# A decoder layer on one core: the down weights of the experts move to ScalarE's queue

## The reference, cut to what matters

```
grp   = argmax of 4 group logits per token
top 2 of the 8 experts of that group, with gates
for each of the 32 experts e, for its rows x:
    hdn = silu(x @ w_gate[e]) * (x @ w_up[e])     # w_gate, w_up: 2048 x 512
    y   = hdn @ w_down[e]                         # w_down: 512 x 2048
out = sum over experts of gate * y, added to the residual; then a final RMSNorm
```

## Time and profile before

| | |
|---|---|
| median of 3 runs | 1797.7 us (1797.01 to 1799.74) |
| span of the profiled execution (the only time it shows of itself) | 1798.1 us |
| PE busy | 1391.6 us, 77% of the span |
| DVE, ACT, POOL busy | 468.6, 281.6, 75.3 us |
| bytes moved | 480.73 MB, of them 474.01 MB on q1 |
| chain that ended last | SPq 41%, PE 40%, DMA 8%, DVE 4% |

### The profile page before, as it was taken

How to read it: one execution, slowest core, us unless ns; L and a number is a source line. 1 busy time by engine, 2 the same in 40 slices (tenths; PEclk the granted TensorE clock), 3 DMA queues, 4 the chain that set the end, 5 groups by cost and what they waited for, 6 DMA issues and landing times.

```text
span 1798.1 us, 20225 instructions
## 1 busy us (share of the span) xinstructions
PE 1391.6 (77%) x7876; PEld 746.3 (42%) x7876; DVE 468.6 (26%) x1007; ACT 281.6 (16%) x602; POOL 75.3 (4%) x107
## 2 busy tenths in 40 slices
PE   4999999999999998887666756755766666766755
PEld 4887878888888544442111211211211211211111
DVE  4031365555554544140111101101101101102003
ACT  2002111111111243121101010110101101010111
POOL 1000011111111400000000000000000000000000
PEclk8999999999999899988887897987978977878787
DMA  8432332222222124959999999999999999999996
GB/s 247 141 116 94 111 88 71 71 70 70 70 70 82 47 94 138 320 190 403 394 398 399 395 402 395 401 396 397 400 395 402 395 399 398 395 401 395 402 395 246
DMA packets 204592, 480.73 MB, mean 267 GB/s; under 512 B 16725, under 2 KB 35302, under 8 KB 187654
## 3 DMA queue, kind: packets, MB, share of 16 engines
q1 hardware_dynamic: 192562, 474.01, 70.8%
q10 hardware_dynamic: 11988, 6.14, 1.4%
HBM read 478.01 MB, written 2.10 MB: 267 GB/s over the span
## 4 chain that ended last, share of the span: by engine, by line
SPq 41%; PE 40%; DMA 8%; DVE 4%; issue 3%; ACTq 2%; ACT 1%; DVEq 0%
SPq L507 20%; SPq L508 15%; PE ps L684 9%; PE ps L756 8%; SPq L512 6%; DMA ring<-in_moe_w_up_dram 6%; PE ps L766 6%; PE ps L901 5%; DMA ring<-in_moe_w_down_dram 2%; PE ps L1015 2%; PE ps L1030 1%; PE ps L989 1%; PE ps L704 1%; PE ps L783 1%; DVE oT L1479 1%
## 5 line engine op out<-in xcount | busy, mean ns | idle before, releaser
L1015 PE MATMUL ps<-ring,oT 128*32 128x512 f32 x2048 | 358.7, 840 | 282.7 <-DMA ring<-in_moe_w_up_dram 282.0
L1015 PEld LDWEIGHTS ps<-ring,oT 128*32 128x32 f32 x2048 | 68.7, 133 | 550.5 <-DMA ring<-in_moe_w_up_dram 317.2
L756 PE MATMUL ps<-xT,ring 128*128 128x256 f32 x768 | 191.5, 386 | 0.0
L684 PE MATMUL ps<-xT,ring 128*128 128x256 f32 x768 | 169.7, 384 | 13.6 <-ACT xT L1144 13.6
L1693 DVE TENSOR_TENSOR oT<-oT,ps 128x128 f32<-128x128 f32 x32 | 9.2, 288 | 643.8 <-ACT oT L1301 643.8
L684 PEld LDWEIGHTS ps<-xT,ring 128*128 128x128 f32 x768 | 147.6, 193 | 35.4 <-issue 15.0
L1030 PE MATMUL ps<-ring,oT 128*32 128x512 f32 x1024 | 123.4, 604 | 48.6 <-DMA ring<-in_moe_w_down_dram 28.6
L756 PEld LDWEIGHTS ps<-xT,ring 128*128 128x128 f32 x768 | 137.6, 193 | 16.6 <-issue 2.7
L1297 ACT COPY oT<-ps 128x512 f32<-128x512 f32 x32 | 18.8, 586 | 648.5 <-PE ps L1015 648.5
L901 PE MATMUL ps<-ring,oT 128*128 128x512 f32 x256 | 118.5, 617 | 1.7 <-DVE oT L1558 0.9
L1030 PEld LDWEIGHTS ps<-ring,oT 128*32 128x32 f32 x1024 | 30.2, 109 | 120.3 <-issue 66.9
(11 more groups left out here) (328 smaller groups left out, 1290.5 us busy)
## 6 DMA issues: line engine op xcount, KB each, us to landing
ring<-in_moe_w_gate_dram SPq DMA_DIRECT2D x128, 1024.0 KB, 14.3
ring<-in_moe_w_up_dram SPq DMA_DIRECT2D x128, 1024.0 KB, 14.4
ring<-in_moe_w_down_dram SPq DMA_DIRECT2D x128, 1024.0 KB, 15.2
ring<-in_w_in_dram SPq DMA_DIRECT2D x24, 1024.0 KB, 5.2
ring<-in_w_in_dram SPq DMA_DIRECT2D x32, 768.0 KB, 4.7
ring<-in_w_out_dram SPq DMA_DIRECT2D x16, 1024.0 KB, 5.1
res<-in_x_dram SPq DMA_DIRECT2D x2, 1024.0 KB, 6.0
out_dram<-oT SPq DMA_DIRECT2D x4, 512.0 KB, 3.0
```

The lines of the kernel that those rows point to most:

```text
L684: last = mm(ps[:, c, 0:S], wv[:, k, c * P:(c + 1) * P], xT[:, kq * KQ + k, :], start=(kq == 0 and k == 0), stop=(kq == 3 and k == KQ - 1))
L756: last = mm(ps[:, 5 + c, 0:S], wv[:, k, c * P:(c + 1) * P], xT[:, kq * KQ + k, :], start=(kq == 0 and k == 0), stop=(kq == 3 and k == KQ - 1))
L1015: last = mm(ps[c * B:(c + 1) * B, 1, :], xe[:, par, 4 * j + k, :], w[:, c // 2, k, :], start=(j == 0 and kp == 0), stop=(j == 3 and kp == ...
```

## The change: what it does

The sync engine keeps the loads of gate and up (chunks 0 to 3) of all experts. Of the down weights it keeps expert 0's (in the first eight chunks) and those of the loop for further tokens. All other down loads are issued by ScalarE: expert n's turn on ScalarE issues the four down loads of expert n+1, between the copy of the partial sums and the copy of the gathered tokens. Slots, semaphores and sizes are the same. The `m_turn` count moves from one chunk of an expert to another, since the sync engine no longer handles chunk 4 there.

```diff
             with sp.Fori(0, 7) as i:
                 for q in range(MSLOTS, MSLOTS + 4 * CHUNKS):
-                    sp.wait_ge(m_read, i * (4 * CHUNKS) + (q - MSLOTS + 1))
-                    if q % CHUNKS == 4:
-                        sp.sem_inc(m_turn, 1)
                     s = (q + LEAD) % MSLOTS
-                    load_chunk(s, bass.ds(i * 4 + q // CHUNKS, 1), q % CHUNKS, m_ring[s])
+                    if q % CHUNKS < 4:
+                        sp.wait_ge(m_read, i * (4 * CHUNKS) + (q - MSLOTS + 1))
+                        if q % CHUNKS == 0:
+                            sp.sem_inc(m_turn, 1)
+                        load_chunk(s, bass.ds(i * 4 + q // CHUNKS, 1), q % CHUNKS, m_ring[s])
             for n in range(MSLOTS + 7 * 4 * CHUNKS, NE * CHUNKS):
-                sp.wait_ge(m_read, n - MSLOTS + 1)
                 s = (n + LEAD) % MSLOTS
-                load_chunk(s, slice(n // CHUNKS, n // CHUNKS + 1), n % CHUNKS, m_ring[s])
+                if n % CHUNKS < 4:
+                    sp.wait_ge(m_read, n - MSLOTS + 1)
+                    load_chunk(s, slice(n // CHUNKS, n // CHUNKS + 1), n % CHUNKS, m_ring[s])
...
+            def next_down(e, u):
+
+                for d in range(2):
+                    s = (CHUNKS * (u + 1) + 4 + d + LEAD) % MSLOTS
+                    at = mslot(s, 2, D).unsqueeze(1)
+                    for f in range(2):
+                        act.dma_start(at[:, :, f:f + 1], wd_t[:, e, 2 * d + f:2 * d + f + 1, :]).then_inc(m_ring[s], 16)
+
             def expert(i, u, last_one):
                 n = i * 4 + u
                 sums(n)
                 if not last_one:
+                    next_down(slice(n + 1, n + 2) if isinstance(n, int) else bass.ds(n + 1, 1), u)
                     tokens(n + 1)
```

## The result

The changed kernel takes 1807.24 us in the median of 4 runs (1804.0 to 1808.88), against 1797.76 us before (1797.01 to 1799.74, 4 runs). The ratio is 1.0053, with an interval of 1.0036 to 1.007: slower by 9.5 us. The forecast was 1804.5 us, with a range of 1795 to 1814.

A forecast was written before the change was run, and what follows sets the result against it. The prediction took weight transfers to bound the expert stage, 31.5 us per expert. Its six terms, all 0 but +6.8 us for the end of the stage, gave a 1804.9 us span and a 1804.5 us time, range 1795 to 1814.

The forecast's parts named there:

- 1. Order of arrival: Expert stage: down weights issued earlier, same bytes, queues never dry together, so the last byte lands when it did; 0 us.
- 2. ScalarE's time: ScalarE's turn per expert: four issues, 2.06 us, delay tokens through down by at most 0.9 us, covered by PE's waiting; 0.
- 3. The sync engine: Sync engine in the expert stage: drops 4 of 12 issues per expert, never the bytes, and is not on the path; 0.
- 4. Start of the stage: Stage opening, first freed slot at 800.80: queued loads leave no gap before the next slot frees at 812.4; cost 0.
- 5. The tail: Stage end: last landing becomes a gate/up chunk, so its matmuls, hidden values and both down chunks follow; +6.8 us.
- 6. The rate with two queues: Expert-stage transfers: queues take turns by packet, costing and saving nothing; 0, bounds +30 and -60 us.
- D: Prediction's name for an expert's two down chunks: 4 loads, 4.19 MB, rows of 8 KB at 426 GB/s.
- G: Prediction's name for an expert's four gate/up chunks: 8 loads, 8.39 MB, rows of 2 KB at 388 GB/s.
- A: Rival, expert stage: mixed queues raise the rate; small 0.24 us per expert, 1797.1, chance 0.18; large 0.96, 1774.5, 0.16.
- C: Rival, expert stage: mixing two streams costs rate, down weights moving at gate/up's rate; +30 us, 1834 us, chance 0.07.
- B: Rival, ScalarE: held in its issues like the sync engine, exceeding the period by 12 us; about +390, 2190 us, chance 0.04.

## Why the prediction was right

The direction, the mechanism and the place of the loss were right: the time in which the weights land is the same, and more work follows the last of them. Point by point:

1. Order of arrival, 0: right. The last chunk is read 973.5 us after the opening, 973.3 before; 973.5 to 974.9 in the four further profiles taken apart above with the old rows. The forecast of the waits was only half right: the 28.6 us for down are gone, but the wait for gate/up grew by 55.9 us and not by about as much.
2. ScalarE's time, 0: right. The issues took 1.89 us against the 2.06 expected, the tokens' copy began 2.14 us behind the sums copy (1.72 before), so 0.4 us later and not 0.9. PE's wait for hidden values is 18.2 us, not more than the 20.0 of the earlier trace rows. Moving the issues out of the way gained nothing.
3. The sync engine, 0: right. It stays in its queue; in the experts shown, its longest issue grew from 8.95 to 11.58 us. One remark of the prediction is a little off: the trace of before has 8.9 us more in which it waited for down chunks to be read, beside the 30.2 us for gate/up.
4. Start of the stage, 0: right, seen by the same 973.5. What the prediction had not reckoned with is that the opening itself wanders between executions, 800.80 to 791.15 in the profiles shown, in a part of the program that the change leaves alone; the single times of the kernel before wander too, 1791.04 to 1801.19 in 22 runs. The traces show part of it. Between the profiles of before and after, 3.9 of the 4.0 us are there at 740, and 1.8 of them are one block of the output projection's matmuls, in before and in after:

```profile
731.49 8.86 PE L901 MATMUL ps<-ring,oT 128*128 128x512 f32 x16
```

```profile
729.44 7.03 PE L903 MATMUL ps<-ring,oT 128*128 128x512 f32 x16
```

From 730 to 750 the granted clock was 0.87 in before and 1.00 in after. Why it differs, and what moved the rest, stays open.
5. The tail, +6.8: right in kind, a little small. It measured 8.0 in the profile of after. Of its terms, from the gate/up chunk to the start of down took 1774.89 - 1770.27 = 4.6 us in place of 5.07: the 5.07 ended in a wait of 1.33 us for down weights, where now down is there and the wait is 0.89 us for the hidden values. The two down chunks took 5.34 in place of 3.64, part of them at the slower clock: 0.55 was granted from 1775 to 1778.

   The differences of the medians, 9.5 and 4.7, lie on both sides of the 6.8; the 14.8 us tail of the swapped kernel lies further up. The prediction had this as the upper part of its own range, 1.7 + 3.6 us, and took the fast clock as its value. That was the mis-sized term. Of the five profiles with gate/up landing last, the down pair took 5.34 us (after), 5.28 (the changed kernel again), 6.02 (chunks swapped) and 5.34 (the change with long rows), and where it took 3.64 (issues moved) the gate/up chunk ahead of it was the slow one: a slow stretch fell into the tail in each. Before, there was one too, the down chunk of 3.60 us at 1769.30, but PE was done with it before the last chunk landed, so it cost nothing.

   One sign of the prediction failed as it was written: point 5 was to be wrong if the last landing came earlier than 1773, and the last chunk was read at 1770.27. The sign was set in time of the span and not from the opening, 4.0 us earlier here; counted from the opening the landing is where it was.
6. The rate with two queues, 0: right. 397 GB/s in the same 200 us that had 399, and the kernel that keeps 120 loads on ScalarE's queue has a ratio of 0.9999. Over the 15 us in which one expert's down weights move, the rate is 410 GB/s before (1033 to 1048) and 410 after (1112 to 1127, shown above).

   How the queues take turns is not shown. If D's 32 packets per engine met 32 of G's, the mix would move 5.24 MB in 4.19/0.426 + 1.05/0.388 = 12.5 us at 418 GB/s; of the five stretches from 1112 to 1127 only two are near that, at 419 and 414, the others have 406, 405 and 408, and the slowest of ScalarE's loads took 17.4 us to land. So D may well get its turns more slowly than one for one. Nor did show it: while those 128 small packets per engine were out, the sync engine issued only two gate/up loads, at 712.01 and 712.42, which are 64 packets per engine, the next at 726.48; and the 0.1 us for 32 KB alone takes the rate of long rows for rows of 16 bytes, which no row shows.

   The forecast of 0 didn't need it: it took every packet to cost the same in any order, and that is what the two means of 410 show. The rule of the Trainium skill, "DMA: Bandwidth & Descriptors", section "Issuing engines are not separate DMA queues", that a second issuer only saves issue time, holds in these runs: with 120 loads on ScalarE's queue the ratio is 0.9999.

Of the rivals, A in both sizes and C fall with the ratio of 0.9999, whose interval leaves no room for 7 us, and with the stage's unchanged 973.8 us. B falls with the 1.89 us. That A had any weight rested on a true observation, the two rates; they belong to the row length, which the change leaves as it is, and not to how many queues carry it.

The prediction's sentence "any faster stage needs a higher rate" was right as well, and it was the useful one: with long rows the higher rate was there to be had, 58 us of it.

## What to carry to other kernels

Where transfers bind a stage, prefetching one of its streams earlier moves waits and, as here, gains nothing; look instead at what lands last, since all work that needs it is added to the end, and put the load with the least work behind it last. Compare parts of the span that begin and end at the same events when an untouched part wanders by as much as the effect. And read GB/s in stretches short enough to tell the streams apart: two levels in one stage point at the shape of the slower stream's rows.

## What the runs showed of the hardware that was not expected

- Rows of 8 KB in place of 2 KB raised the stage's loads to a steady 422 GB/s, where gate/up alone had run at 388; the DMA share fell from 1.04 to 1.01.
- The sync engine's queue held more bytes with longer rows. The gate loads took 14.3 us to land with rows of 2 KB and 26.2 with rows of 8 KB, at a higher rate. The row of the kernel with long rows:

```profile
ring<-in_moe_w_gate_dram SPq DMA_DIRECT2D x128, 1024.0 KB, 26.2
```

  26.2 us at 422 GB/s are 11.1 MB, 14.3 us at 388 are 5.5 MB. If a load's time to land is taken as what stands in the queue ahead of it, these are estimates of how much the queue held. So what fills the queue is not bytes alone.
- A matmul whose moving operand is read with a stride of 16 float32 elements took 1033 ns in the median, the same matmul with adjacent elements 592.
- With long rows on the changed kernel the sync engine no longer stood in its queue alone: it waited 86.4 us for gate/up and 51.1 us for down chunks to be read (38.9 and 0.5 in the changed kernel with the old rows), and the stage kept 421 to 422 GB/s all the same.
